# A kernel of two transformer blocks on one core: the order of rope, outputs and first projections in the second block's mixers, and the output's second quarter

## The chip, the cores and the metric

The kernel runs on one core of one Trainium2 chip. It is one program for five engines that work side by side and wait for each other through semaphores: TensorE (PE in the profile) multiplies matrices, VectorE (DVE) and ScalarE (ACT) do the elementwise work, GpSimd (POOL) does a little of it, and SyncE (SP) starts the transfers. The metric is the time of one execution on the device in microseconds, taken as the median of several runs.

## What is computed

The input is 256 tokens of width 1024 in fp32. A first block applies, each with a norm and a modulation, a feed-forward net (width 2816), a mixer (half pooling, half attention with ALiBi) and a second such net. A second block has two attention mixers with rotary embedding (rope), grouped keys and a gate z: one with a window of 128 and sinks, one that for 256 tokens is plain causal attention. The parts that the change touches:

```python
def second_block(x, norm_g, w_in_a, sinks_a, w_in_b, w_out, final_g):
...
    for i in range(DEPTH_2):
        hn = rmsnorm_2(h, norm_g[i])
        j = i // N_MIXERS
        if i % N_MIXERS == 0:
            q, k, v, z = split_proj(hn, w_in_a[j], N_KV_A)
            q, k = apply_rope(q, cos, sin), apply_rope(k, cos, sin)
            o = sliding_window_sink_attention(q, k, v, sinks_a[j])
        else:
            q, k, v, z = split_proj(hn, w_in_b[j], N_KV_B)
            q, k = apply_rope(q, cos, sin), apply_rope(k, cos, sin)
            o = moba_attention(q, k, v)
        o = o.reshape(B, S, MIX_WIDTH) * jax.nn.silu(z)
        h = h + o @ w_out[i]
    return rmsnorm_2(h, final_g)
```

## The kernel before

**Split products.** fp32 accuracy is had from three fast products. Each operand is a high part (`whi`, `nhi`, `yhi`: a rounded copy made by ScalarE) and a low part (`wlo`, `nlo`, `ylo`: the difference, made by VectorE). `split_product` issues hi x hi, hi x lo and lo x hi, so a chunk of 128 rows costs three matmuls with 256 columns.

**Weight units.** Weights come as units of 1024 x 256 (1 MB, `load_unit`, L412) into three slots. For each unit ScalarE makes the high half (`high`, L599) and VectorE the low half (`low`, L907); the next load into a slot waits for the low half of its unit. Units are numbered in the order in which they are used; a call `low(u + NS)` prepares the unit three places on. Queues are in order: an engine that waits holds up all that is behind it.

**The plan.** `mixer_plan` writes out for each mixer ("pool", "window", "causal") a list of steps, and each engine walks the same list and does its part of each step:

- K, KV, V, Q, Z, U, W: projections ("jobs") of a unit into the bank `acc[p % 2]`, 48 matmuls on TensorE; ScalarE copies the bank out (`kraw`, `vv`, `qraw`, tanh of z) and counts `job_out`.
- ROTK, ROTQ: TensorE multiplies with the rotation matrix (`rotate`, L1503 and L1506), VectorE combines with cosine and sine (`rope`, L1063 to L1067) and counts `rope_done`. For keys ScalarE then spreads the heads (`duplicate`, L709) and counts `kd_done`.
- SC: the scores of four heads (L1522, L1523), maxima on VectorE (`masked_max`, L1081), exponentials on ScalarE (L725), divisions on VectorE (`divide`, L1101). Between them lie the scaling and the gating of z (L1182, L1188). At the end ScalarE makes a high half and VectorE its low half.
- TPV: transposes of the probabilities (L1532), copies by ScalarE (`probT`, L732), products with the values (L1546, L1549), and for two pairs of heads `og` on VectorE (L1114), `yhi` on ScalarE (L743), `ylo` on VectorE (L1119) (`outputs`). ScalarE ends the step with a high half.
- OUTA, OUTB, OUT1 to OUT3: the output projection in four quarters. OUTA is chunks 0 to 5 of the first quarter, done before the last TPV, OUTB its chunks 6 and 7 after it. OUT1 to OUT3 are whole quarters of 48 matmuls. After each quarter VectorE adds the residual (L918 or L921), and in "window" ScalarE and VectorE make `nhi`, `sq` and `nlo` (L947) of the next mixer's input.
- ROW, MOD (only "pool"): parts of the modulation vector; ROW29 is a matrix row that VectorE copies (L1013) and MOD28 sums.

For the second and third mixer the order before is

```
window: KV0 Q0 ROTK ROTQ Z0 SC0      causal: K0 V0 Q0 ROTK ROTQ Z0 SC0
both:   for i in 1..3: Q(i) TPV(i-1) ROTQ Z(i) SC(i);  OUTA TPV3 OUTB OUT1 OUT2 OUT3
```

TensorE does the first half of Z, two heads' scores, then the second half, and the other two heads' scores. It also does the transposes of two heads in the middle of the next Q, and the rotation inside TPV. In "window" VectorE also computes the first block's final norm in place, as one reciprocal after SC0 (`plain_inverse`, L967) and four chunks each after SC1 and SC2 (`first_output`, L972). `token_columns` (TensorE) and `token_column` (VectorE, `rcol`) turn the norm's factors into columns, by which ScalarE scales the values `vv`.

## Time and profile before

| | |
|---|---|
| median of the runs | 813.81 us (811.53 to 816.93, 3 runs) |
| the profiled execution, its time | 816.46 us |
| the profiled execution, its span | 814.7 us |
| TensorE busy | 743.1 us, 91% |
| VectorE busy | 544.3 us, 67% |
| ScalarE busy | 367.9 us, 45% |
| GpSimd busy | 128.5 us, 16% |
| mean granted clock of TensorE | 0.951 of full speed |

"pool" runs from about 250 to 362 us of the span, "window" from 560 to 682, "causal" from 682 to the end. A busy time is the sum of an engine's instructions; matmuls overlap, so a busy TensorE need not be at its peak. The timeline lists instructions by their start with their length; a number in brackets at a row's end is the idle time of the engine just before it and the instruction that ended that idle time. The granted clock is a share of 2.4 GHz.

### The profile page before, as it was taken

How to read it: one execution, taken by the hardware profiler on the slowest of the kernel's cores; microseconds unless marked ns; L12 is line 12 of the kernel's file. 1: busy time of each engine (PE TensorE's matmuls, PEld its weight loads, DVE VectorE, ACT ScalarE, POOL GpSimd, SP SyncE). 2: the span in 40 equal slices, each digit the busy share in tenths (PEclk: the TensorE clock that was granted, in tenths of full speed). 3: DMA queues.
4: the chain of work that ended last, by engine and by line, in shares of the span. 5: the costliest groups of instructions: out<-in, count | busy, mean ns of one | idle time of the engine just before them, and what ended most of it. 6: DMA issues, size and time to landing. Idle time of an engine off the chain costs nothing.

```text
span 814.7 us, 14918 instructions
## 1 busy us (share of the span) xinstructions
PE 743.1 (91%) x6112; PEld 693.3 (85%) x6112; DVE 544.3 (67%) x783; ACT 367.9 (45%) x564; POOL 128.5 (16%) x81
## 2 busy tenths in 40 slices
PE   5799999999978998879999999999988889899984
PEld 4489999999967987669999999999877769787884
DVE  3598978877767348466478457456888856577841
ACT  3253434343434345425443434438655556356532
POOL 0052213222241805030004000004000000000000
PEclk9699999999978999798999999999999979899998
DMA  9987799777657965354667656554333315434201
GB/s 312 349 277 256 239 367 298 235 246 242 221 180 225 342 225 166 104 188 126 204 207 257 206 158 203 180 180 132 127 105 104 104 53 179 134 103 135 72 2 51
DMA packets 132455, 152.64 MB, mean 187 GB/s; under 512 B 2616, under 2 KB 126268, under 8 KB 132284
## 3 DMA queue, kind: packets, MB, share of 16 engines
q1 hardware_dynamic: 132324, 152.01, 57.5%
q8 instruction: 31, 0.51, 0.3%
q14 instruction: 12, 0.10, 0.0%
q10 hardware_dynamic: 88, 0.02, 0.0%
HBM read 150.97 MB, written 1.05 MB: 187 GB/s over the span
## 4 chain that ended last, share of the span: by engine, by line
PE 37%; DVE 9%; ACT 7%; issue 4%; DVEq 0%; ACTq 0%
PE sc L1336 5%; PE sc L1338 5%; PE sc L1337 5%; PE acc L1336 5%; PE acc L1338 5%; PE acc L1337 5%; ACT whi L599 2%; ACT prob L725 1%; DVE prob L1081 1%; DVE wlo L907 1%; PE acc L1589 1%; ACT probT L732 1%; PE acc L1591 1%; PE acc L1590 1%; PE stat L1347 1%
## 5 line engine op out<-in xcount | busy, mean ns | idle before, releaser
L907 DVE TENSOR_TENSOR wlo<-raw,whi 128x2048 fp32r<-128x2048 f32 x105 | 260.8, 2487 | 121.1 <-ACT whi L599 120.9
L599 ACT ACTIVATE whi<-raw 128x2048 fp32r<-128x2048 f32 x105 | 200.2, 1908 | 74.7 <-PE sc L1338 56.7
L1336 PE MATMUL sc<-nhi,whi 128*128 128x256 f32 x704 | 200.0, 284 | 6.0 <-DVE nlo L940 4.1
L1337 PE MATMUL sc<-nlo,whi 128*128 128x256 f32 x704 | 198.5, 282 | 0.0
L1338 PE MATMUL sc<-nhi,wlo 128*128 128x256 f32 x704 | 198.4, 282 | 0.0
L1336 PEld LDWEIGHTS sc<-nhi,whi 128*128 128x128 f32 x704 | 134.0, 190 | 7.4 <-issue 4.5
L1337 PEld LDWEIGHTS sc<-nlo,whi 128*128 128x128 f32 x704 | 135.6, 193 | 0.0
L1338 PEld LDWEIGHTS sc<-nhi,wlo 128*128 128x128 f32 x704 | 134.4, 191 | 0.0
L1336 PE MATMUL acc<-nhi,whi 128*128 128x256 f32 x376 | 112.8, 300 | 3.1 <-DVE nlo L940 2.7
L517 POOL TENSOR_TENSOR ada<-ada,cpad 128x2048 f32<-128x2048 f32 x16 | 73.0, 4569 | 243.0 <-DMA ada<-in_w_ada_dram 243.0
L1337 PE MATMUL acc<-nlo,whi 128*128 128x256 f32 x376 | 107.3, 285 | 0.0
L1338 PE MATMUL acc<-nhi,wlo 128*128 128x256 f32 x376 | 107.3, 285 | 0.0
L1336 PE MATMUL acc<-hhi,whi 128*128 128x256 f32 x320 | 89.7, 280 | 0.0
L1337 PE MATMUL acc<-hlo,whi 128*128 128x256 f32 x320 | 89.6, 280 | 0.0
L1338 PE MATMUL acc<-hhi,wlo 128*128 128x256 f32 x320 | 89.6, 280 | 0.0
L1336 PEld LDWEIGHTS acc<-nhi,whi 128*128 128x128 f32 x376 | 74.1, 197 | 12.9 <-issue 10.5
L1337 PEld LDWEIGHTS acc<-nlo,whi 128*128 128x128 f32 x376 | 74.1, 197 | 0.6 <-issue 0.5
L1338 PEld LDWEIGHTS acc<-nhi,wlo 128*128 128x128 f32 x376 | 73.8, 196 | 0.0
L983 DVE TENSOR_REDUCE macc<-ada 128x256 f32<-128x2048 f32 x16 | 61.5, 3863 | 3.5 <-POOL ada L517 3.5
L1337 PEld LDWEIGHTS acc<-hlo,whi 128*128 128x128 f32 x320 | 60.9, 190 | 0.0
L1338 PEld LDWEIGHTS acc<-hhi,wlo 128*128 128x128 f32 x320 | 60.3, 189 | 0.0
L1336 PEld LDWEIGHTS acc<-hhi,whi 128*128 128x128 f32 x320 | 60.1, 188 | 0.0
(209 smaller groups left out, 1162.5 us busy)
## 6 DMA issues: line engine op xcount, KB each, us to landing
ada<-in_w_ada_dram SPq DMA_DIRECT2D x28, 1024.0 KB, 5.2
raw<-in_w_gate_dram SPq DMA_DIRECT2D x22, 1024.0 KB, 5.9
raw<-in_w_up_dram SPq DMA_DIRECT2D x22, 1024.0 KB, 5.6
raw<-in_w_down_dram SPq DMA_DIRECT2D x22, 1024.0 KB, 4.9
raw<-in_w_out_dram SPq DMA_DIRECT2D x12, 1024.0 KB, 5.1
raw<-in_w_in_b_dram SPq DMA_DIRECT2D x10, 1024.0 KB, 5.1
raw<-in_w_in_a_dram SPq DMA_DIRECT2D x9, 1024.0 KB, 5.3
raw<-in_w_in_dram SPq DMA_DIRECT2D x8, 1024.0 KB, 7.8
```

Of the source, the lines that this page charges most:

```text
L517: nc.gpsimd.tensor_tensor(to, to, c_mul, ALU.mult).then_inc(prod_done, 1)
L599: nc.scalar.activation(whi[:, u % NS], raw[:, u % NS], ACT.Copy).then_inc(hi_done, 1)
L725: ins = nc.scalar.activation(prob[:, s, lo:up], prob[:, s, lo:up], ACT.Exp, bias=nm[:, s, b:b + 1], accum_out=den[:, s, b:b + 1])
L732: nc.scalar.activation(probT[:, h % 2], tp[h % 2][:, 0:SW], ACT.Copy).then_inc(pt_done, 1)
L907: nc.vector.tensor_tensor(wlo[:, u % NS], raw[:, u % NS], whi[:, u % NS].bitcast(F32), ALU.subtract).then_inc(lo_done, 1)
L983: nc.vector.tensor_reduce(macc[:, slot], ada[:, slot].rearrange("p c n -> p n c"), AX_X, ALU.add).then_inc(macc_done, 1)
L1081: ins = nc.vector.tensor_tensor_reduce(out=prob[:, s, lo:up], in0=sc[h % 2][:, lo:up], in1=mask[:, lo:up], scale=1.0, scalar=NEG, op0=ALU. ...
L1336: mm(to, stat_hi, mov_hi, start=first, stop=False, skip_group_check=True)
L1337: mm(to, stat_hi, mov_lo, start=False, stop=False, skip_group_check=True)
L1338: return mm(to, stat_lo, mov_hi, start=False, stop=last, skip_group_check=True)
L1347: mm(ss_ps, ones[:, :], src, start=first, stop=last).then_inc(ss_done, 1)
L1589: mm(to, yhi[:, ch, tok], hi[:, ch], start=False, stop=False, skip_group_check=True)
```

## The change

It has four parts.

1. The rope of queries that follows a TPV step stands on VectorE ahead of that step's outputs instead of behind them. The low half that followed the rope (`low(query["u"] + NS)`) stands in SC after the first two maxima. In "window" the reciprocal and the rescaling stand ahead of SC's last low half instead of behind it.
2. "window" begins KV0 ROTK Q0 ROTQ: the key rotation waits on a semaphore of its own (`k_out`, counted by the copy of the keys), and VectorE's rope of the keys stands ahead of `rcol` and the low half.
3. "causal" begins K0 Q0 ROTK V0 ROTQ: units Q0 and V0 are exchanged, the token columns move into V0, and two low halves stand behind the query's rope.
4. A new step OUTC, chunks 0 to 5 of the output's second quarter, stands between OUTA and the last TPV in all three mixers. OUT1 keeps chunks 6 and 7.

```diff
@@ mixer_plan
-                     "MOD26", "ROW28", "W0", "W1", "V1", "SC0", "Q1", "TPV0", "SC1", "OUTA", "TPV1", "OUTB", "ROW29",
+                     "MOD26", "ROW28", "W0", "W1", "V1", "SC0", "Q1", "TPV0", "SC1", "OUTA", "OUTC",
+                     "TPV1", "OUTB", "ROW29",
...
-            order = ["KV0", "Q0"] if name == "window" else ["K0", "V0", "Q0"]
-            order += ["ROTK", "ROTQ", "Z0", "SC0"]
+            order = ["KV0", "ROTK", "Q0"] if name == "window" else ["K0", "Q0", "ROTK", "V0"]
+            order += ["ROTQ", "Z0", "SC0"]
...
-            order += ["OUTA", "TPV3", "OUTB", "OUT1", "OUT2", "OUT3"]
+            order += ["OUTA", "OUTC", "TPV3", "OUTB", "OUT1", "OUT2", "OUT3"]
...
-                st["rcol"] = name != "pool" and kind == "Q" and i == 0
+                st["rcol"] = kind == {"pool": "", "window": "Q", "causal": "V"}[name] and i == 0
@@ scalar: job, mixer
-                    nc.scalar.activation(kraw[:, 0], bank[:, 0:S], ACT.Copy)
+                    nc.scalar.activation(kraw[:, 0], bank[:, 0:S], ACT.Copy).then_inc(k_out, 1)
...
-                    elif st["kind"] == "ROTK":
+                    elif st["kind"] == "ROTK" and name == "causal":
                         duplicate(st)
+                    elif st["kind"] == "ROTQ" and name == "window" and before["kind"] == "Q":
+                        duplicate(PLANS[name][1])
@@ vector: mixer
-                    if kind == "V" and name == "causal" or kind == "Q" and name == "window" and st["rcol"]:
+                    if st.get("rcol"):
                         token_column(MIX_NORM[name])
+                        if name == "window":
+                            low(st["u"] - 1 + NS)
                     if st.get("first") and name != "pool":
                         token_scales(MIX_NORM[name])
-                    if st.get("job"):
+                    if kind == "KV" or kind == "V" and name == "causal":
+                        pass
+                    elif st.get("job"):
                         job(st)
-                    elif kind in ("ROTK", "ROTQ"):
+                    elif kind == "ROTK":
                         rope(st)
-                        if kind == "ROTQ":
-                            low(query["u"] + NS)
+                    elif kind == "ROTQ" and query["i"] == 0:
+                        rope(st)
+                        low(query["u"] + NS)
+                        if name == "causal":
+                            low(query["u"] + 1 + NS)
                     elif kind == "SC":
                         masked_max(st, 0)
                         masked_max(st, 1)
+                        if before["kind"] == "Z" and before["i"]:
+                            low(query["u"] + NS)
...
+                        if name == "window" and before["i"] == 0:
+                            plain_inverse()
+                        elif name == "window" and before["i"] < 3:
+                            first_output(range(4 * before["i"] - 4, 4 * before["i"]))
                         low((before if before["kind"] in ("Z", "V") else query)["u"] + NS)
-                        if name == "window":
-                            if before["i"] == 0:
-                                plain_inverse()
-                            elif before["i"] < 3:
-                                first_output(range(4 * before["i"] - 4, 4 * before["i"]))
                     elif kind == "TPV":
+                        if st["next"]["kind"] == "ROTQ":
+                            rope(st["next"])
                         outputs(st)
@@ tensor: out_step
-                    if kind == "OUT" and st["zs_all"]:
+                elif kind == "OUTC":
+                    pe.wait_ge(lo_done, st["u"] + 1)
+                    pe.wait_ge(job_out, st["jobs"])
+                    if st["zs_all"]:
                         pe.wait_ge(z_done, st["zs_all"])
...
-                if kind == "OUTB":
-                    out_product(st, 0, 0, late, False, True).then_inc(delta, 1)
-                    out_product(st, 0, 1, late, False, True).then_inc(delta, 1)
+                if kind == "OUTC":
+                    out_product(st, 1, 0, early, True, False)
+                    out_product(st, 1, 1, early, False, False)
+                    return
+                if kind == "OUTB" or j == 1:
+                    out_product(st, j, 0, late, False, True).then_inc(delta, 1)
+                    out_product(st, j, 1, late, False, True).then_inc(delta, 1)
```

How the instructions move is seen in each engine's queue. VectorE in "window", from the last division of SC2 on to the next scores, before:

```order
L1101 TENSOR_SCALAR prob<-prob,rden 128x256
L907 TENSOR_TENSOR wlo<-raw,whi 128x2048 [waits hi_done]
L972 SCALAR_TENSOR_TENSOR hT<-hT,gainT,sq 128x256 x4
L1114 SCALAR_TENSOR_TENSOR og<-acc,sz 128x256 [waits ylo_done,pv_done]
L1119 TENSOR_TENSOR ylo<-og,yhi 128x256 [waits yhi_done]
L1114 SCALAR_TENSOR_TENSOR og<-stat,sz 128x256 [waits ylo_done,pv_done]
L1119 TENSOR_TENSOR ylo<-og,yhi 128x256 [waits yhi_done]
L1063 TENSOR_TENSOR tn<-qraw,sq 128x512 [waits rope_done,job_out]
L1066 TENSOR_TENSOR tn<-sc,sq 128x512 [waits rot_done]
L1067 TENSOR_TENSOR qT<-tn 128x512 [waits dve_step]
L907 TENSOR_TENSOR wlo<-raw,whi 128x2048 [waits hi_done]
L1081 ISA prob,mx<-sc,consts 128x128 [waits sc_done]
```

and the same place after the change, where the second low half comes ten rows on, behind the second maximum (line numbers are those of the changed file):

```order
L1108 TENSOR_SCALAR prob<-prob,rden 128x256
L976 SCALAR_TENSOR_TENSOR hT<-hT,gainT,sq 128x256 x4
L911 TENSOR_TENSOR wlo<-raw,whi 128x2048 [waits hi_done]
L1070 TENSOR_TENSOR tn<-qraw,sq 128x512 [waits rope_done,job_out]
L1073 TENSOR_TENSOR tn<-sc,sq 128x512 [waits rot_done]
L1074 TENSOR_TENSOR qT<-tn 128x512 [waits dve_step]
L1121 SCALAR_TENSOR_TENSOR og<-acc,sz 128x256 [waits ylo_done,pv_done]
L1126 TENSOR_TENSOR ylo<-og,yhi 128x256 [waits yhi_done]
L1121 SCALAR_TENSOR_TENSOR og<-stat,sz 128x256 [waits ylo_done,pv_done]
L1126 TENSOR_TENSOR ylo<-og,yhi 128x256 [waits yhi_done]
L1088 ISA prob,mx<-sc,consts 128x128 [waits sc_done]
```

The rescaling (`hT`) went ahead of the low half, and the three instructions of the rope ahead of the four of the outputs. VectorE at the start of "causal", from the sine table on, before:

```order
L957 TENSOR_TENSOR sq<-consts,rstd 128x256 [waits dve_step]
L907 TENSOR_TENSOR wlo<-raw,whi 128x2048 [waits hi_done,dve_step]
L962 COPY rcol<-stat 128x2 [waits rcol_sum]
L907 TENSOR_TENSOR wlo<-raw,whi 128x2048 [waits hi_done]
L1063 TENSOR_TENSOR tn<-kraw,sq 128x512 [waits rope_done,job_out]
L1066 TENSOR_TENSOR tn<-sc,sq 128x512 [waits rot_done]
L1067 TENSOR_TENSOR kraw<-tn 128x512 [waits dve_step]
L1063 TENSOR_TENSOR tn<-qraw,sq 128x512 [waits rope_done,job_out]
L1066 TENSOR_TENSOR tn<-sc,sq 128x512 [waits rot_done]
L1067 TENSOR_TENSOR qT<-tn 128x512 [waits dve_step]
L907 TENSOR_TENSOR wlo<-raw,whi 128x2048 [waits hi_done]
```

and after:

```order
L961 TENSOR_TENSOR sq<-consts,rstd 128x256 [waits dve_step]
L911 TENSOR_TENSOR wlo<-raw,whi 128x2048 [waits hi_done,dve_step]
L1070 TENSOR_TENSOR tn<-kraw,sq 128x512 [waits rope_done,job_out]
L1073 TENSOR_TENSOR tn<-sc,sq 128x512 [waits rot_done]
L1074 TENSOR_TENSOR kraw<-tn 128x512 [waits dve_step]
L966 COPY rcol<-stat 128x2 [waits rcol_sum]
L1070 TENSOR_TENSOR tn<-qraw,sq 128x512 [waits rope_done,job_out]
L1073 TENSOR_TENSOR tn<-sc,sq 128x512 [waits rot_done]
L1074 TENSOR_TENSOR qT<-tn 128x512 [waits dve_step]
L911 TENSOR_TENSOR wlo<-raw,whi 128x2048 [waits hi_done] x2
```

One low half went from ahead of the keys' rope to behind the queries'. TensorE at the end of "window", where the last product of OUTA is followed by the transposes of TPV3, before:

```order
L1338 MATMUL acc<-yhi,wlo 128x256
L1532 MATMUL tp<-consts,prob 128x128 [waits pt_done,p_done]
L1532 MATMUL tp<-consts,prob 128x128 x2
L1532 MATMUL acc<-consts,prob 128x128 [waits pt_done,p_done]
L1532 MATMUL acc<-consts,prob 128x128 x2
L1546 MATMUL acc<-probT,vv 64x256 [waits og_done,pt_done]
```

and after, the end of OUTA and the first rows of OUTC, which has 36 such rows ahead of the same transposes:

```order
L1355 MATMUL acc<-yhi,wlo 128x256
L1353 MATMUL acc<-yhi,whi 128x256 [waits z_done,job_out,lo_done]
L1354 MATMUL acc<-ylo,whi 128x256
L1355 MATMUL acc<-yhi,wlo 128x256
L1353 MATMUL acc<-yhi,whi 128x256
```

The 36 products came from OUT1, behind OUTB, and took its wait for `z_done` with them.

## Rows read from the trace of the kernel before

**Rows 1.** Busy time by stretch: stretch, length, PE, PEld, DVE, ACT, POOL, granted clock, DMA
```profile
620.00:660.00 40.00, 31.79 (x242) 26.77 (x244) 31.96 (x97) 22.24 (x58) 0.00 (x0) 0.91 0.27 89
...
740.00:780.00 40.00, 37.02 (x307) 31.45 (x306) 31.71 (x88) 23.52 (x53) 0.00 (x0) 1.00 0.24 80
...
648.20:652.40 4.20, 4.20 (x38) 4.20 (x37) 4.06 (x19) 2.35 (x10) 0.00 (x0) 1.00 0.47 164
...
601.00:605.30 4.30, 4.30 (x27) 3.97 (x25) 3.73 (x14) 1.60 (x8) 0.00 (x0) 0.60 0.30 89
...
656.20:666.50 10.30, 9.23 (x44) 7.24 (x45) 4.36 (x9) 4.46 (x10) 0.00 (x0) 0.52 0.32 103
```

**Rows 2.** Timeline of TensorE, matmuls behind the waits that concern the change
```profile
622.14 0.40 PE L1522 MATMUL sc<-kd,qT 64*128 64x128 f32 x2 [2.56 <-DVE qT L1067]
...
748.21 0.39 PE L1522 MATMUL sc<-kd,qT 64*128 64x128 f32 x2 [1.17 <-DVE qT L1067]
...
656.16 0.44 PE L1546 MATMUL acc<-probT,vv 128*64 128x256 f32 x2 [2.94 <-ACT probT L732]
...
328.29 0.44 PE L1546 MATMUL acc<-probT,vv 128*64 128x256 f32 x2 [3.78 <-ACT probT L732]
...
705.70 1.19 PE L1506 MATMUL sc<-qraw,consts 128*128 128x512 f32 x1 [3.50 <-issue]
```

**Rows 3.** Timeline of VectorE, a turn of its loop in "window"
```profile
613.79 2.29 DVE L907 TENSOR_TENSOR wlo<-raw,whi 128x2048 fp32r<-128x2048 f32 x1 [1.61 <-ACT whi L599]
616.00 1.67 DVE L972 SCALAR_TENSOR_TENSOR hT<-hT,gainT,sq 128x256 f32<-128x256 f32 x4
617.58 0.42 DVE L1114 SCALAR_TENSOR_TENSOR og<-acc,sz 128x256 f32<-128x256 f32 x1
...
620.07 0.69 DVE L1063 TENSOR_TENSOR tn<-qraw,sq 128x512 f32<-128x512 f32 x1
...
622.00 2.28 DVE L907 TENSOR_TENSOR wlo<-raw,whi 128x2048 fp32r<-128x2048 f32 x1
...
635.18 2.29 DVE L907 TENSOR_TENSOR wlo<-raw,whi 128x2048 fp32r<-128x2048 f32 x1 [1.61 <-ACT whi L599]
```

**Rows 4.** Timeline of VectorE, a turn of its loop in "causal"
```profile
741.45 2.29 DVE L907 TENSOR_TENSOR wlo<-raw,whi 128x2048 fp32r<-128x2048 f32 x1 [1.80 <-ACT whi L599]
...
746.15 0.69 DVE L1063 TENSOR_TENSOR tn<-qraw,sq 128x512 f32<-128x512 f32 x1
...
748.08 2.28 DVE L907 TENSOR_TENSOR wlo<-raw,whi 128x2048 fp32r<-128x2048 f32 x1
...
759.89 2.29 DVE L907 TENSOR_TENSOR wlo<-raw,whi 128x2048 fp32r<-128x2048 f32 x1 [1.80 <-ACT whi L599]
```

**Rows 5.** Timeline of ScalarE, the high half behind the outputs in "causal"
```profile
745.68 1.90 ACT L599 ACTIVATE whi<-raw 128x2048 fp32r<-128x2048 f32 x1
```

**Rows 6.** Timeline of VectorE, residuals of two output quarters in "window"
```profile
671.24 0.76 DVE L918 TENSOR_TENSOR hT<-acc,hT 128x256 f32<-128x256 f32 x2 [0.36 <-PE acc L1338]
...
677.34 0.75 DVE L918 TENSOR_TENSOR hT<-acc,hT 128x256 f32<-128x256 f32 x2
```

**Rows 7.** Timeline of VectorE and GpSimd behind the outputs of "pool"
```profile
336.70 0.88 DVE L921 SCALAR_TENSOR_TENSOR hT<-acc,mod,hT 128x256 f32<-128x256 f32 x2 [2.38 <-PE acc L1338]
...
342.07 0.42 DVE L1013 COPY macc<-tp 128x256 f32<-128x256 f32 x1
...
347.69 5.26 DVE L907 TENSOR_TENSOR wlo<-raw,whi 128x2048 fp32r<-128x2048 f32 x1 [2.29 <-ACT whi L599]
...
347.18 3.62 POOL L517 TENSOR_TENSOR ada<-ada,cpad 128x2048 f32<-128x2048 f32 x1
```

**Rows 8.** Timeline of VectorE at the start of "window"
```profile
571.62 2.29 DVE L907 TENSOR_TENSOR wlo<-raw,whi 128x2048 fp32r<-128x2048 f32 x1
573.83 0.15 DVE L962 COPY rcol<-stat 128x2 f32<-128x2 f32 x1
```

**Rows 9.** Timeline of TensorE, the first scores of "causal"
```profile
712.05 0.39 PE L1522 MATMUL sc<-kd,qT 64*128 64x128 f32 x2
```

50 lines of the change are left out of this document (30 added, 20 removed).

## The prediction

> **What bounds the kernel now.** I read the busy shares of stretches first. While the heads of the two later mixers run, TensorE is busy 79 to 93% and VectorE 79 to 80% [rows 1]: no engine is full, so what matters is the chain of waits. Its pieces alternate there between VectorE and ScalarE, and TensorE shows only as the one that waits at its end. Next I read the timeline of TensorE for the longest idle times [rows 2]. Five kinds concern this change: the scores of a group of heads wait 2.6 us for `qT` in "window" (three such waits, 2.8, 2.6, 2.6) and 0.5 to 1.2 us in "causal" (three); the first value products of `TPV3` wait 2.94 us for `probT` in "window", those of `TPV1` in "pool" 3.78 us; and the rotation of the first queries in "causal" waits 3.50 us. Behind the longest of these the granted clock fell to the lower of its two levels, 1.2 GHz: it is 0.52 of full speed over 656.2 to 666.5 and 0.60 over 601.0 to 605.3, where 27 matmuls took 4.3 us, against 38 in 4.2 us at full clock [rows 1]. A wait of 2.6 us brought this in one of two places, 2.8 and more each time.
>
> Then I asked what `qT` waits for, in the timeline of VectorE [rows 3, 4]. One turn of its loop in "window" is: the low half of weights (2.29), the rescaled residual (1.67), two outputs each with a round trip to ScalarE (2.5), the rope (1.95), another low half (2.3), four maxima and divisions. The next turn begins 21.4 us later (613.79 and 635.18). In "causal" without the rescaling it is 18.44 us (741.45 to 759.89). Inside a turn VectorE stands still for 1.6 to 1.8 us until ScalarE has made the high half [rows 3, 4] and shorter at some other places. So the loop is VectorE and ScalarE in series, and TensorE's waits are its symptom. This decides the sum: taking a wait from TensorE gives its full length only where the loop gets shorter as well.
>
> **The heads of "window".** Two things move. The rescaling (1.67 us, twice; once a reciprocal of 1.75) now stands ahead of the low half, where VectorE idled 1.61 us [rows 3]: its cover is the high half on ScalarE, and if that cover were gone it would cost its 1.67 us again. The rope stands ahead of the outputs, so `qT` is ready 2.2 + 1.95 = 4.2 us behind the start of the low half, instead of 8.3 (613.79 to the scores at 622.14). TensorE then has the rotation (it needs `qraw`, which follows the high half), the value products (0.9) and half of Z (2.8) to do, and reaches the scores about 5.1 us after the low half began, without a wait: the 2.6 us are gone. The outputs come 1.95 us later. Behind them, on ScalarE, are `yhi`, a high half of 1.9 us and then the exponentials [rows 5]. And the low half of the next-but-one weights stands between the maxima and the first division. It waits for that high half, which ends about when the maxima end (outputs + 0.3 + 1.9 against outputs + 1.6): no new wait of more than 0.5. The turn is then 2.2 + 1.95 + 2.55 + 1.5 + 2.3 + the rest of 8.3 (21.4 less all these and about 1 us of waits) = 18.8 us: 2.6 less per full turn. From the first rope on I get: scores of the second group 3.1 us earlier, the loop behind it 2.8 earlier, 5.4 after the second turn and 7.6 when ScalarE begins the high half ahead of `probT` of the fourth. So this part gives 7.6.
>
> **The last wait of "window".** `OUTC` is 36 products. 38 take 4.2 us [rows 1], so it is 4.1 us. It starts once Z3 is gated, which is about when `OUTA` ends, and it lies in the 3.7 us that TensorE now spends on transposes and waiting [rows 2]: transposes and `probT` then cost 0.4 us of lateness. Without a wait of 2.9 us the clock should stay at 2.4 GHz: now 44 matmuls behind it keep TensorE busy for 9.2 us at 0.52 [rows 1]; they would need about half, of which the round trips to ScalarE and VectorE hide part, so I take 2.5 us as the gain. Together: 7.6 - 0.4 + 2.5 = 9.7 us at the end of `OUTB`. `OUT1` then has 12 products, 1.4 us, instead of 48, 5.5 us. But this does not give 4.1 us. Each output quarter costs VectorE and ScalarE 6.1 us in series (residual 671.24, next 677.34 [rows 6]), TensorE only 5.5. The first projection of "causal" needs the last `nlo`, which comes 3 x 6.1 + 2.2 us behind the first residual: 21.4 us from `OUTB` to its end, against 22.8 now (4 x 48 matmuls at 5.5 and some of them at the lower clock). So 1.4 us, and TensorE waits about 2.8 us in K0 instead. Sum up to K0: **11.1**.
>
> **"pool".** `OUTC` fills the 3.78 us, and the clock should hold: `OUTB` ends 2.3 us earlier with 4.1 us of `OUT1` done. Here too something else is late next. `MOD28` needs the copied row of `ROW29`, which VectorE makes 5.4 us behind the residual's start (336.70 and 342.07 [rows 7]); TensorE comes there 2.3 us after `OUTB` and waits 3.6. After that VectorE's next low half again meets GpSimd's product (5.26 us instead of 2.29, [rows 7]) and `ROW31` waits behind it as before. By this chain `ROW31` is at 349.5 instead of 353.5: **3.8**. That VectorE and GpSimd hinder each other is in the row; the Trainium skill, "GPSIMD Engine Reference", section "Specifications", says that GpSimd shares its SBUF interfaces with VectorE and contends with VectorE instructions of two SBUF inputs; by that rule the collision comes again, and the trace agrees (5.26 us). If it fell away, `ROW31` would wait for the end of `OUT2` alone and the term would be 5.7.
>
> **First keys and queries.** In "window" the low half (2.29) stood ahead of the copy of `rcol`, for which ScalarE's `vv` and so the rotation waited [rows 8]. Now the rope of the keys (1.3) stands there instead, and the rotation of the keys runs ahead of Q0. Of the 2.3 us the rope takes 1.3 back, so ROTQ starts earlier by **1.0**. In "causal" TensorE now does V0 between the two rotations. The key rope no longer stands behind a second low half, so it ends at about 697.4, long before V0 does, and the query's rotation follows V0 without the 3.50 us [rows 2]. Counted from the end of K0, the scores come at 705.1 instead of 712.05 [rows 9]: 6.9 for TensorE, 1.6 of it for the clock. VectorE however has two low halves (4.5 us) behind the query's rope, so the maxima start at 708.4 instead of 713.0, which is 1 us behind the scores: 4.6 for the loop. The turns of "causal" have no rescaling to hide; permuted, they take 18.15 us against 18.44, two turns give 0.6. At the last group's scores the rope's new place helps TensorE once, 1.6 us (scores 5.15 us behind the low half instead of 6.77). 4.6 + 0.6 + 1.6 = 6.8, and 0.2 for the end, where `OUTC` meets only waits of 0.6 to 0.9 us inside the attention step, which stay. **7.0**.
>
> **Sum.** 3.8 + 1.0 + 11.1 + 7.0 = 22.9. Against it one dropped clock at K0 or MOD28: 27 matmuls in 4.3 us, which take 3.0 at 38 in 4.2 [rows 1], is a loss of 1.3; at somewhat better than even odds I take 0.9. That leaves 22.0 off a span of 814.7, an execution of 816.46: 794.5. This execution lay 0.3% above the median of the runs, 813.81; on that the forecast is **792**.
>
> **Bounds.** Lower bound of the gain: only what TensorE's first two parts give and nothing in the loops (3.8 + 1.0 + 1.4 + 4.6 less two clock drops of 1.3) is 8. Upper: every wait above gone with its clock loss, 8.0 + 2.9 + 3.8 + 3.5 + 2.8 + 1.2, and 6.9 for the clock in four stretches (1.3 in a short one, 2.5 in the longest) is 29.
>
> **Rivals.** A: TensorE is the bound and the waits go in full, 29 us, about 785. For it: TensorE has the largest busy share. Against it: VectorE's turn, which barely gets shorter in "causal". The Trainium skill, "Perfetto Trace Analysis", section "Identifying the Most-Contended Engine", tells one to work on the engine of the highest occupancy; by that rule the whole 29 us would come. The rows on VectorE's turn speak against it. Chance 0.08.
> B: the loop in "window" doesn't shorten by 2.6 a turn but by under 1, because the high half ahead of the exponentials (1.9 us, [rows 5]) is late and VectorE's low half and division wait for it; TensorE's wait moves to the transposes. Then the loops give 3 instead of 7.6 and the clock still drops: gain 9 to 15, 799 to 805. Chance 0.15.
> C: within 1%: B, and the 4.6 of "causal" are not reached because the two low halves wait for their high halves; gain 4 to 8, about 808. Chance 0.08.
> D: slower. The one mechanism is that same low half ahead of the first division: it makes all six groups wait for ScalarE's high half in series with the exponentials. It decides once it adds over 3.5 us to each turn, over seven groups 24 us and more; by the rows it is 0.1 to 0.5. About 822. Chance 0.03.
> The forecast itself, 787 to 799, has 0.66. The range of 785 to 804 takes in most of A and B. From the cases: faster by over 1% 0.88, within 1% 0.09, slower 0.03; 1% is about what a measurement of this kernel tells from no change.
>
> **What would show it.** Right: in "window" no wait for `qT` over 0.5 us and 18.8 us from one low half behind the divisions to the next, 18.1 in "causal"; no granted clock of 0.5 in the last heads of "pool" and "window"; a new wait of about 3.6 us at `MOD28` and one near 2.8 us in K0. Wrong: turns still of 21 us, or an idle VectorE ahead of the low half that now precedes the first division. If K0's wait is missing, my 6.1 us per quarter was not the bound there.

## The result, and the profile after

| | before | after |
|---|---|---|
| median of the runs | 814.54 us (811.53 to 816.93, 4 runs) | 796.50 us (795.86 to 796.62, 4 runs) |
| the profiled execution, its time | 816.46 us | 795.86 us |
| its span | 814.7 us | 793.9 us |
| TensorE busy | 743.1 us, 91% | 733.2 us, 92% |
| VectorE busy | 544.3 us, 67% | 542.9 us, 68% |
| mean granted clock | 0.951 | 0.970 |

After to before is 0.9765 (95% interval 0.9737 to 0.9792): the change makes the kernel 2.3% faster. The forecast was 792 us with a range of 785 to 804, so it lies 4.5 us low and the range holds the time. On the profiled executions, against which the sum was made, the forecast was 794.5 and the time is 795.86. (The median before, 814.54, is of the three runs behind the 813.81 and one more.)

The table below cuts both spans at the same instructions. Each number is the difference of two start times in the timeline of TensorE: the first product of ROW28 ("pool"), the first product behind "pool", the first sum of squares of "window", the first scores of SC0 and of SC3, the first sum of squares behind OUT3 of "window" (the end of K0), the first scores of "causal", its SC3, and the end of the span. The 0.9 us that was forecast for a dropped clock has a row of its own; where a clock did drop, its cost lies in the row of its stretch.

| stretch, us | before | after | gained | forecast |
|---|---|---|---|---|
| start to ROW28 (nothing changed) | 296.07 | 296.54 | -0.5 | 0 |
| ROW28 to the end of "pool" | 71.39 | 68.08 | 3.3 | 3.8 |
| up to "window" (nothing changed) | 198.43 | 198.40 | 0.0 | 0 |
| first projections of "window" | 14.72 | 13.73 | 1.0 | 1.0 |
| "window", SC0 to SC3 | 62.92 | 54.71 | 8.2 | |
| SC3 to the end of K0 | 43.83 | 42.00 | 1.8 | |
| both together | 106.75 | 96.71 | 10.0 | 11.1 |
| end of K0 to the scores of "causal" | 24.69 | 18.55 | 6.1 | |
| "causal", SC0 to SC3 | 54.61 | 53.98 | 0.6 | |
| SC3 to the end | 48.04 | 47.91 | 0.1 | |
| these three together | 127.34 | 120.44 | 6.9 | 7.0 |
| a dropped clock | | | | -0.9 |
| span | 814.7 | 793.9 | 20.8 | 22.0 |

The busy shares by stretch, of after. Columns: stretch, length, PE, PEld, DVE, ACT, POOL, granted clock, DMA share, GB/s.

```profile
600.00:640.00 40.00, 37.53 (x309) 32.05 (x308) 36.21 (x113) 23.77 (x62) 0.00 (x0) 1.00 0.37 123
720.00:760.00 40.00, 38.86 (x319) 33.52 (x318) 31.84 (x90) 23.42 (x54) 0.00 (x0) 1.00 0.25 80
340.90:346.40 5.50, 5.47 (x32) 4.19 (x33) 3.22 (x3) 2.55 (x3) 4.40 (x3) 0.50 0.01 3
...
650.80:655.00 4.20, 4.20 (x36) 4.20 (x37) 1.72 (x4) 3.38 (x7) 0.74 (x1) 1.00 0.04 12
```

and, of before, the stretch that lies to the last scores of "window" as the first row does:

```profile
612.00:652.00 40.00, 34.89 (x276) 29.57 (x275) 32.52 (x93) 21.33 (x53) 0.00 (x0) 0.96 0.32 106
```

In the heads of "window" VectorE is now busy 91% of the time and TensorE 94% at full clock; before it was 81% and 87%. (The 80% and 79% of [rows 1] are of a stretch that reaches into the last attention step.) Behind the last attention step of "window" the clock is 1.00 (last row of after), where it was 0.52 [rows 1]. It is down behind MOD28, for 32 matmuls in 5.5 us (third row).

The timeline of VectorE, of after, one turn in "window" and the marks of a turn in "causal" (they answer [rows 3, 4]):

```profile
603.83 0.55 DVE L1108 TENSOR_SCALAR prob<-prob,rden 128x128 f32<-128x128 f32 x2
604.77 0.16 DVE L1105 TENSOR_TENSOR den<-den,esink 128x2 f32<-128x2 f32 x1 [0.40 <-ACT prob L727]
...
605.63 1.67 DVE L976 SCALAR_TENSOR_TENSOR hT<-hT,gainT,sq 128x256 f32<-128x256 f32 x4
607.32 2.29 DVE L911 TENSOR_TENSOR wlo<-raw,whi 128x2048 fp32r<-128x2048 f32 x1
609.53 0.68 DVE L1070 TENSOR_TENSOR tn<-qraw,sq 128x512 f32<-128x512 f32 x1
...
611.46 0.42 DVE L1121 SCALAR_TENSOR_TENSOR og<-acc,sz 128x256 f32<-128x256 f32 x1
612.36 0.43 DVE L1126 TENSOR_TENSOR ylo<-og,yhi 128x256 fp32r<-128x256 f32 x1 [0.48 <-ACT yhi L745]
...
615.57 2.28 DVE L911 TENSOR_TENSOR wlo<-raw,whi 128x2048 fp32r<-128x2048 f32 x1
...
626.17 2.29 DVE L911 TENSOR_TENSOR wlo<-raw,whi 128x2048 fp32r<-128x2048 f32 x1
...
722.66 2.29 DVE L911 TENSOR_TENSOR wlo<-raw,whi 128x2048 fp32r<-128x2048 f32 x1 [1.80 <-ACT whi L601]
...
740.69 2.29 DVE L911 TENSOR_TENSOR wlo<-raw,whi 128x2048 fp32r<-128x2048 f32 x1 [1.80 <-ACT whi L601]
```

The low half at 607.32 has no bracket: the rescaling fills what was a wait of 1.61 us [rows 3]. The rope stands between it and the first output, and the turn's second low half, at 615.57, waits for nothing. From 607.32 to 626.17 a turn is 18.85 us, before 21.39. In "causal", with nothing to put into the wait of 1.80, it is 18.03 against 18.44.

The timeline of TensorE, of after, the waits that stand where those of [rows 2] stood, and two new ones:

```profile
646.18 0.65 PE L1568 MATMUL acc<-probT,vv 128*64 128x256 f32 x4 [0.63 <-ACT probT L734]
...
329.11 0.65 PE L1568 MATMUL acc<-probT,vv 128*64 128x256 f32 x4 [0.63 <-ACT probT L734]
...
612.62 0.50 PE L1544 MATMUL sc<-kd,qT 64*128 64x128 f32 x4
...
340.93 1.01 PE L1383 MATMUL acc<-ones,macc 128*128 128x1 f32 x4 [2.93 <-DVE macc L1017]
...
671.94 0.38 PE L1353 MATMUL acc<-nhi,whi 128*128 128x256 f32 x1 [2.35 <-DVE nlo L951]
```

The waits for `probT` went from 2.94 and 3.78 to 0.63 each, no scores wait for `qT`, and no row of "causal" has the 3.50 us. In their place TensorE waits 2.93 us at MOD28 and 2.35 us in K0; 3.6 and 2.8 were forecast.

### The profile page after: what moved, and what is told of

Its sections match the earlier page's. It is cut to its first block, busy times and chain, and to the rows that moved or that the text cites. A ratio compares the mean times of both kernels' runs of the same rounds, so it can differ in the third digit from the quotient of the medians.

```text
span 793.9 us, 14919 instructions
## 1 busy us (share of the span) xinstructions
PE 733.2 (92%) x6112; PEld 685.8 (86%) x6112; DVE 542.9 (68%) x783; ACT 366.6 (46%) x564; POOL 128.7 (16%) x81
## 4 chain that ended last, share of the span: by engine, by line
PE 68%; DVE 15%; ACT 10%; issue 4%; DMA 2%; POOL 0%; SPq 0%; DVEq 0%; ACTq 0%; POOLq 0%
PE sc L1353 10%; PE sc L1355 10%; PE sc L1354 10%; PE acc L1353 9%; PE acc L1355 8%; PE acc L1354 8%; DVE wlo L911 5%; ACT whi L601 3%; PE stat L1364 2%; DVE prob L1088 2%; DMA ada<-in_w_ada_dram 2%; ACT probT L734 1%; PE tp L1404 1%; ACT prob L727 1%; DVE prob L1108 1%
## 5 line engine op out<-in xcount | busy, mean ns | idle before, releaser
L911 DVE TENSOR_TENSOR wlo<-raw,whi 128x2048 fp32r<-128x2048 f32 x105 | 258.2, 2463 | 113.1 <-ACT whi L601 112.9
L1353 PE MATMUL acc<-nhi,whi 128*128 128x256 f32 x376 | 110.8, 295 | 5.6 <-DVE nlo L944 2.7
L1354 PE MATMUL acc<-nlo,whi 128*128 128x256 f32 x376 | 105.6, 281 | 0.0
L1355 PE MATMUL acc<-nhi,wlo 128*128 128x256 f32 x376 | 105.5, 281 | 0.0
L1353 PEld LDWEIGHTS acc<-nhi,whi 128*128 128x128 f32 x376 | 72.0, 191 | 15.2 <-issue 10.2
L1354 PEld LDWEIGHTS acc<-nlo,whi 128*128 128x128 f32 x376 | 72.1, 192 | 0.3 <-issue 0.2
L1355 PEld LDWEIGHTS acc<-nhi,wlo 128*128 128x128 f32 x376 | 71.9, 191 | 0.0
```

The source lines that it names most:

```text
L911: nc.vector.tensor_tensor(wlo[:, u % NS], raw[:, u % NS], whi[:, u % NS].bitcast(F32), ALU.subtract).then_inc(lo_done, 1)
L1353: mm(to, stat_hi, mov_hi, start=first, stop=False, skip_group_check=True)
L1354: mm(to, stat_hi, mov_lo, start=False, stop=False, skip_group_check=True)
L1355: return mm(to, stat_lo, mov_hi, start=False, stop=last, skip_group_check=True)
```

## The experiments

Eleven kernels were run, in three sessions, each session with its own runs of the kernel before (medians 816.67, 816.32 and 813.44 us). Ratios are to those, with a 95% interval. Stretches are those of the table above, each from one profiled execution. Part 2 was not run alone; its 1.0 us is read from the first projections of "window", which take 14.71 to 14.81 us in every kernel without it and 13.73 to 13.90 in every kernel with it.

**One part at a time.** The kernel before with part 4 alone:

```diff
-            order += ["OUTA", "TPV3", "OUTB", "OUT1", "OUT2", "OUT3"]
+            order += ["OUTA", "OUTC", "TPV3", "OUTB", "OUT1", "OUT2", "OUT3"]
...
```

> The kernel before with the new step OUTC alone (part 4). Theory (VectorE and ScalarE in series are the bound): in 'pool' OUTC fills the wait of 3.78 us, MOD28 then waits about 3.1 us as in the changed kernel, gain 3.0; in 'window' the wait of 2.94 us and the low clock behind it go, and K0 waits about 2.4 us, gain 5; in 'causal' 0.2. Together 8 us, ratio 0.990. Rival (all moved work is gained, 3 x 4.1, and the clock with it): 16 us, ratio 0.980. The waits of 2.6 us for qT and of 3.50 us at the first rotation of 'causal' stay.

Measured: 808.14 us, 0.9943 (0.9904 to 0.9981). Its ten times lie apart, six from 806.56 to 808.83 and four from 812.96 to 816.23, and the profiled one is among the six, so its stretches show more than the ratio does. The profiled span, 805.4, is 9.3 shorter than that of before: 4.2 from ROW28 to the end of "pool", 1.3 in the unchanged stretch behind it, 0.6 in "window", 1.75 from SC3 to the end of K0, 1.2 behind K0, where 4 matmuls run at the low clock instead of 16, and nothing at the end. The waits for `qT` stay at 2.81 and 2.54 us. Of the 5 us expected in "window" little came: OUTC alone is worth its waits in "pool" and less where the loop of VectorE sets the pace. In all, 8 us were expected; by the ratio, 0.990 lies just outside the interval.

With part 1 alone:

```diff
...
+                        if before["kind"] == "Z" and before["i"]:
+                            low(query["u"] + NS)
...
                     elif kind == "TPV":
+                        if st["next"]["kind"] == "ROTQ":
+                            rope(st["next"])
                         outputs(st)
```

The rescaling goes ahead of the low half as well, as in the change.

> The kernel before with part 1 alone (rope ahead of the outputs, the low half behind two maxima, the rescaling ahead of the low half). Theory: a turn of VectorE's loop in 'window' is 18.9 us instead of 21.4, in 'causal' 18.1 instead of 18.44; the scores no longer wait for qT; gain 7.3 in 'window' and 2.2 in 'causal', 9.5 us, ratio 0.988. The wait for probT behind OUTA and its low clock stay. Rival (TensorE is the bound, its waits for qT and the clock behind them go in full): 13.4 us, ratio 0.9835, with a turn in 'causal' of 17.1 us.

Measured: 809.35 us, 0.9918 (0.9889 to 0.9946), where 0.988 was expected; the profiled span, 809.5, is 5.2 shorter than that of before. "window" from SC0 to SC3 is 54.70 instead of 62.92 us, which is all of the 8.2 of the whole change. "causal" gets 1.5 shorter in its heads. But the last attention steps give back 1.0 and 2.0 us, so that up to K0 the 7.3 us come as expected and "causal" as a whole gives nothing instead of 2.2: SC3 to K0 takes 44.78 (43.83 before) and SC3 to the end 50.00 (48.04). The timeline of TensorE and the busy shares there, of this kernel:

```profile
650.22 0.65 PE L1550 MATMUL acc<-probT,vv 128*64 128x256 f32 x4 [3.89 <-ACT probT L732]
...
772.24 0.65 PE L1550 MATMUL acc<-probT,vv 128*64 128x256 f32 x4 [1.14 <-ACT probT L732]
...
656.50:661.20 4.70, 4.70 (x23) 4.70 (x23) 1.72 (x4) 2.90 (x7) 0.68 (x1) 0.50 0.00 0
776.90:780.70 3.80, 3.80 (x20) 3.80 (x20) 0.00 (x0) 1.90 (x1) 0.00 (x0) 0.56 0.00 0
```

A faster TensorE ahead of the last step waits longer in it (3.89 us instead of 2.94), and in "causal" a new wait of 1.14 us is followed, 4 us later, by 20 matmuls in 3.8 us at a clock of 0.56. From these rows I concluded that OUTC was worth 2 us in "causal" beside part 1, ten times the 0.2 of the prediction. That was tested below and fell.

With part 3 alone:

```diff
-            order = ["KV0", "Q0"] if name == "window" else ["K0", "V0", "Q0"]
-            order += ["ROTK", "ROTQ", "Z0", "SC0"]
+            order = ["KV0", "Q0", "ROTK"] if name == "window" else ["K0", "Q0", "ROTK", "V0"]
+            order += ["ROTQ", "Z0", "SC0"]
...
```

> The kernel before with part 3 alone (K0 Q0 ROTK V0 ROTQ in 'causal'). Theory: the first scores come 6.1 us earlier behind K0, but the maxima only 4.1 us earlier, since VectorE has two low halves behind the rope, and the loop carries 4.1 us to the end: ratio 0.995. Rival (TensorE's path counts): the 6.1 us reach the end, ratio 0.9925.

Measured: 813.66 us, 0.9977 (0.9954 to 1.0000). The scores come 6.3 us earlier behind K0 (18.36 instead of 24.69), and 1.65 of it is gone at SC3 (56.26 instead of 54.61). So 4.7 us reach the last scores: near the loop's 4.1, not TensorE's 6.1. The profiled span is only 3.3 shorter, since 0.8 was lost between SC3 and K0 and 0.6 ahead of ROW28, which the edit does not touch. The ratio shows less still, 1.9 us, and the expected 0.995 is not in its interval: that 4.7 us reach the last scores is seen in one execution, and the times alone do not show it.

**Who sets the pace.** Leave out a third of TensorE's products in the projections Q1 to Q3 and Z1 to Z3 of both mixers, 192 of them or 21.7 us, in the kernel before and in the changed one. It is the product of the weights' low part and the input's high part (the first expectation below names another); `light` is set in these projections alone, and VectorE still makes the low part:

```diff
                 mm(to, stat_hi, mov_hi, start=first, stop=False, skip_group_check=True)
+                if light[0]:
+                    return mm(to, stat_hi, mov_lo, start=False, stop=last, skip_group_check=True)
```

> The kernel before with a third of the matmuls left out of the projections Q1 to Q3 and Z1 to Z3 of 'window' and 'causal' (the product of high part and low part of the input), so its numbers are a little coarser: 16 of 48 matmuls in each of 12 units, 192 in all, 21.7 us of TensorE at full clock. Theory: the loop of VectorE and ScalarE sets the turns, which stay at 21.4 and 18.44 us less at most 0.4; TensorE's waits grow by what is left out, and more of it runs at the low clock. Gain under 4 us, ratio 0.995 to 1.0. Rival (TensorE is the bound): 20 us or more, ratio 0.975.

> The changed kernel with the same 192 matmuls left out as in the light version of the kernel before (a third of the projections Q1 to Q3 and Z1 to Z3 of 'window' and 'causal'). Theory: after the change too the loop of VectorE and ScalarE sets the turns, 18.9 and 18.1 us; gain on the changed kernel under 3 us, ratio to the kernel before 0.974 to 0.977. Rival (the change made TensorE the bound of these turns): 15 us or more, ratio 0.958.

Measured: 815.44 us, 0.9988 (0.9958 to 1.0018) for the one, 795.82 us, 0.9748 (0.9709 to 0.9787) for the other. The work that is gone turns up as waiting. The timeline of TensorE, kernel before with less TensorE work:

```profile
602.29 0.50 PE L1525 MATMUL sc<-kd,qT 64*128 64x128 f32 x4 [4.03 <-DVE qT L1067]
...
623.24 0.50 PE L1525 MATMUL sc<-kd,qT 64*128 64x128 f32 x4 [3.88 <-DVE qT L1067]
```

and the changed kernel with less TensorE work:

```profile
603.27 0.55 PE L1557 MATMUL acc<-consts,prob 128*128 128x128 f32 x3 [0.90 <-DVE prob L1108]
607.45 0.65 PE L1571 MATMUL acc<-probT,vv 128*64 128x256 f32 x4 [1.80 <-ACT probT L734]
```

The wait for `qT` grows from 2.6 to 4 us; in the changed kernel the wait is for `prob` and `probT` instead. SC0 to SC3 of "window" takes 61.96 (62.92) and 53.81 us (54.71). TensorE has the largest busy share in both kernels and bounds neither of these stretches; rival A of the prediction rested on it being the bound. That ScalarE is in the loop beside VectorE is read from VectorE's waits for it and from the next experiment; no run shortened ScalarE's own work.

**The rescaling.** The changed kernel, with reciprocal and rescaling behind the low half again:

```diff
-                        if name == "window" and before["i"] == 0:
-                            plain_inverse()
-                        elif name == "window" and before["i"] < 3:
-                            first_output(range(4 * before["i"] - 4, 4 * before["i"]))
                         low((before if before["kind"] in ("Z", "V") else query)["u"] + NS)
+                        if name == "window":
+                            if before["i"] == 0:
+                                plain_inverse()
+                            elif before["i"] < 3:
+                                first_output(range(4 * before["i"] - 4, 4 * before["i"]))
```

> The changed kernel with one thing undone: reciprocal and rescaling of 'window' (1.75, 1.67, 1.67 us on VectorE) stand behind the low half again. Theory: they lay in VectorE's wait for ScalarE's high half and lose that cover, so three turns get longer by 1.6 us each, 5 us in all, ratio 0.9825. Rival (the gain came from the rope's place alone, the rescaling is hidden either way): under 1 us, ratio 0.9765.

Measured: 801.49 us, 0.9812 (0.9777 to 0.9847). SC0 to SC3 of "window" takes 58.47 us instead of 54.71. The timeline of VectorE of this kernel has the wait back:

```profile
612.28 2.29 DVE L911 TENSOR_TENSOR wlo<-raw,whi 128x2048 fp32r<-128x2048 f32 x1 [1.60 <-ACT whi L601]
614.49 1.67 DVE L976 SCALAR_TENSOR_TENSOR hT<-hT,gainT,sq 128x256 f32<-128x256 f32 x4
```

3.8 us for three places, where 5 were expected from the 1.6 to 1.7 us of each in the row: of the 8.2 us of "window", nearly half is this one exchange. The other half goes with the places of rope and second low half, which were not moved one by one. The rest of this execution's loss (2.2 us in the unchanged feed-forward stretch, 1.0 ahead of ROW28) is not from the edit; that of 1.0 between SC3 and K0 was not traced.

**MOD28.** The changed kernel, with the copy of the matrix row ahead of the low half behind OUTB, and the same for the next row:

```diff
+                        if name == "pool" and kind == "OUTB":
+                            copy_late_row(29)
+                        elif name == "pool" and st["i"] == 1:
+                            mod_out(28)
+                            copy_late_row(30)
                         if st["i"] < 3 or name == "causal":
                             low(st["u"] + NS)
...
```

> The changed kernel, and in 'pool' VectorE copies the rows of ROW29 and ROW30 and takes the sums of MOD28 before its low half of the same step, in its wait for the high half. Theory: the wait of 3.1 us at MOD28 goes and the low clock behind it too, but VectorE's residuals and low halves, one of them held up by GpSimd's product, end the stretch: gain 1 to 2 us. Rival (TensorE's wait counts in full with its clock): 4 us. Third: nothing, as the last residual is as late as before.

Measured: 796.54 us, 0.9777 (0.9748 to 0.9807), the time of the changed kernel, as the third of the expected cases had it. The wait at MOD28 is gone and ROW28 to the end of "pool" is the same 68.06 us. The timelines of VectorE, GpSimd and TensorE of this kernel say why:

```profile
342.28 5.25 DVE L911 TENSOR_TENSOR wlo<-raw,whi 128x2048 fp32r<-128x2048 f32 x1 [1.90 <-ACT whi L601]
...
350.62 5.15 DVE L911 TENSOR_TENSOR wlo<-raw,whi 128x2048 fp32r<-128x2048 f32 x1 [2.30 <-ACT whi L601]
...
350.00 3.62 POOL L519 TENSOR_TENSOR ada<-ada,cpad 128x2048 f32<-128x2048 f32 x1 [4.61 <-DMA ada<-in_w_ada_dram]
...
356.16 1.02 PE L1388 MATMUL sc<-ones,macc 128*128 128x1 f32 x4 [4.04 <-DVE macc L1017]
```

and of after, the same two low halves and the same two products of GpSimd:

```profile
343.94 5.25 DVE L911 TENSOR_TENSOR wlo<-raw,whi 128x2048 fp32r<-128x2048 f32 x1 [2.28 <-ACT whi L601]
...
343.42 3.62 POOL L519 TENSOR_TENSOR ada<-ada,cpad 128x2048 f32<-128x2048 f32 x1
...
353.90 2.29 DVE L911 TENSOR_TENSOR wlo<-raw,whi 128x2048 fp32r<-128x2048 f32 x1 [2.29 <-ACT whi L601]
...
357.02 3.62 POOL L519 TENSOR_TENSOR ada<-ada,cpad 128x2048 f32<-128x2048 f32 x1 [9.98 <-DMA ada<-in_w_ada_dram]
```

In both kernels the first product meets a low half. The second waits for the transfer of its matrix, and in this kernel it starts at 350.00 instead of 357.02, seven microseconds earlier, so the next low half meets it as well: 5.15 us instead of 2.29. (That the transfer is earlier because VectorE gave back its buffer earlier was not tested.) The saved time comes back as a wait of 4.04 us at MOD30.

**OUTC, mixer by mixer.** The changed kernel, with OUTC taken out of "causal" alone, and out of "window" alone (OUT1 is whole there again):

```diff
-            order += ["OUTA", "OUTC", "TPV3", "OUTB", "OUT1", "OUT2", "OUT3"]
+            order += ["OUTA"] + (["OUTC"] if name not in ('causal',) else []) + ["TPV3", "OUTB", "OUT1", "OUT2", "OUT3"]
```

> The changed kernel, with OUTC taken out of "causal" alone (OUT1 is whole there again); "pool" and "window" keep it. Theory: OUTC fills TensorE's waits inside the last attention step of "causal", which moving the rope has lengthened, and keeps the clock up there. The stretch from the last scores to the end of the span is then 49.9 instead of 47.9 us, as in the kernel with part 1 alone (50.0), and the kernel is 2.0 us slower than the changed one: ratio to the kernel before about 0.979. Rival, the prediction's own step: OUTC is worth 0.2 there, since the waits stay; the stretch is 48.1 and the ratio stays at 0.9765. All other stretches as in the changed kernel to 0.3 us in both theories.

> The changed kernel, with OUTC taken out of "window" alone; "pool" and "causal" keep it. Theory: in "window" OUTC is worth 2.8 us beside part 1, as the difference of the stretches from the last scores to the sums of K0 (44.78 with part 1 alone, 42.00 with the change) says; the stretch is 44.8 here, the wait for probT is back at about 3.9 us, the wait for the last low half of the input in K0 is gone or under 0.5, and the ratio is about 0.980. Rival A: OUTC is worth what it gave alone on the kernel before (1.75 us in this stretch): 43.75 and 0.9785. Rival B, the prediction's figures (transposes and probT cost 0.4, clock 2.5 and quarters 1.4): 3.5 us, 45.5 and 0.981.

Measured without it in "causal": 797.24 us, 0.9800 (0.9783 to 0.9816); SC3 to the end takes 48.54 us, against 47.91 with OUTC (within 0.2 of it in every other kernel that has both OUTC and part 1) and 50.00 with part 1 alone. The timeline of TensorE and the busy shares of this kernel, in the places of the second and fourth row of part 1 alone:

```profile
757.52 0.65 PE L1568 MATMUL acc<-probT,vv 128*64 128x256 f32 x4 [1.15 <-ACT probT L734]
...
762.20:766.00 3.80, 3.80 (x32) 3.80 (x33) 0.55 (x1) 1.92 (x1) 0.00 (x0) 1.00 0.00 0
```

The wait is the same, 1.15 us against 1.14, and the clock holds: 32 matmuls in 3.8 us where it was 20. So of the 2.0 us in part 1 alone about 0.5 was work and the rest a clock that fell in that execution. My theory of 2.0 us falls; OUTC is worth 0.6 in this stretch, and the prediction's 0.2 was closer. Medians can't settle so little here (0.9800 and 0.9765 have intervals that overlap).

Without it in "window": 797.78 us, 0.9802 (0.9786 to 0.9819); SC3 to K0 takes 45.50 us instead of 42.00. That is 3.5 us, as by the prediction's own terms (rival B of the expectation). But single executions spread: with OUTC and the same code in this stretch it also took 42.17, 42.68 and 43.00 us (the last two with a clock that fell in K0), and 44.78 without OUTC in part 1 alone. So OUTC is worth 2 to 3.5 us there, and the ratio, with 0.980 and 0.981 both in its interval, does not tell the theory's 2.8 from 3.5. The wait of the input's low half in K0 is gone, and its place is taken by the wait and the clock of before, in the timeline of TensorE and the busy shares of this kernel:

```profile
646.59 1.12 PE L1568 MATMUL acc<-probT,vv 128*64 128x256 f32 x4 [3.88 <-ACT probT L734]
...
653.50:658.50 5.00, 5.00 (x25) 5.00 (x25) 1.72 (x4) 3.21 (x7) 0.73 (x1) 0.51 0.00 0
```

**Filling the waits that are left.** With one low half of "causal" moved ahead of the rope of the first queries, where VectorE waited 4.71 us:

```diff
+                    elif kind == "V" and name == "causal":
+                        low(query["u"] + NS)
...
-                        low(query["u"] + NS)
-                        if name == "causal":
+                        if name == "window":
+                            low(query["u"] + NS)
+                        else:
                             low(query["u"] + 1 + NS)
```

> The changed kernel, with one low half in "causal" moved from behind the rope of the first queries to ahead of it, into the 4.7 us in which VectorE waits for the rotation of these queries; nothing else. Theory: the first maxima come one low half (2.3 us) earlier, but the scores stand only 3 us ahead of them and the loop behind takes part of it back, so the stretches from K0 to the last scores lose 1.1 us as they did when all fills were made together: ratio about 0.975. Rival: they lose 2.1 us, and in the kernel with all fills it was another fill that took 1 us back: ratio about 0.974, with 52 us from the first to the last scores of "causal" instead of 53.98.

Measured: 793.06 us, 0.9747 (0.9731 to 0.9764). SC0 to SC3 of "causal" takes 52.91 us, 1.1 less, as the theory had it. In this execution the scores came 0.8 later behind K0 (19.31 us), where the clock was down for some matmuls, so the profile shows a gain of 0.2 over all of "causal"; the ratio shows 0.2% with intervals that overlap.

And with this fill, the copies of the MOD28 experiment, and a low half behind the last `nlo` of "window" instead of ahead of it:

```diff
+                            if st["i"] == 3:
+                                low(st["u"] - 1 + NS)
...
-                        if st["i"] < 3 or name == "causal":
+                        if st["i"] < 3 and (name, st["i"]) != ("window", 2) or name == "causal":
                             low(st["u"] + NS)
```

> The changed kernel with three low halves or copies moved into waits: the row copies of 'pool' as in the run that does them alone; in 'window' the low half of the third output step stands behind the last input low parts, which takes 2.3 us out of the chain to K0's last chunk; in 'causal' the low half of Q1's weights stands ahead of the query's rope, where VectorE waited 4.7 us for the rotation. Theory (VectorE and ScalarE in series): K0's wait of 2.35 us goes, 2.3 us; the first maxima of 'causal' come 2.1 us earlier and the loop carries it; with 1 to 2 of 'pool' 6 us in all, ratio 0.969. Rival (the waits move on): under 2 us, ratio 0.975.

Measured: 793.50 us, 0.9726 (0.9703 to 0.9749), profiled span 790.1. SC3 to K0 takes 39.57 us instead of 42.00, since the quarter that set the 6.1 us no longer has a low half in it; "causal" gets 1.1 shorter in its heads; "pool" nothing. The theory had 6 us and 0.969, outside the interval: 2.1 in "causal" and 1 to 2 in "pool" were too much. By ratio and by span it is the fastest kernel of the study, 3.8 us under the changed one by the profiled spans and 3.0 by the medians; against the kernel with the one fill, 0.9747, the intervals overlap.

## Why the prediction was right

**The bound.** Right. The pace of the heads is set by VectorE and its waits for ScalarE; 21.7 us less work on TensorE changed the time by 0.1%, within the interval, in the one kernel and by as little in the other.

**The heads of "window".** The turn was to be 18.8 us and is 18.95 and 18.85, as part 1 alone also has it. When ScalarE begins the high half ahead of the last `probT` the loop is 7.3 us ahead of where it was, counted from the first scores; 7.6 was the term. What was said to hide the rescaling does hide it. (The prediction's addends of the turn come to 18.8 only if the 1.67 of the rescaling is taken off the 21.4 too, which it does not say.)

**The last wait of "window".** The mechanism was right, its parts a little large. At the residual of OUTB the gain is 8.8 us where 9.7 was forecast, and at the end of K0 10.0 where it was 11.1. The mis-sized term is the clock: I took half of a stretch with 44 matmuls, 2.5 us. Counted in the timeline of before, 19 matmuls there follow each other at the low clock with 0.1 us more than at the full one, which is 1.9. The quarters were as forecast: residuals at 652.15, 658.18, 664.26 and 670.35, 6.03 to 6.1 us apart, and TensorE waits for the last `nlo`. From the first residual to the end of K0 it takes 21.31 us instead of 22.59, a gain of 1.3 for the forecast 1.4 (the prediction's 21.4 names only 3 x 6.1 + 2.2 = 20.5 of its addends).

**"pool".** 3.3 us instead of 3.8 (by the prediction's own 353.5 and 349.5 for ROW31 it would be 4.0). The wait at MOD28 came (2.93 instead of 3.6), and behind it the low half of 5.25 us beside GpSimd's product. That this is a chain that gives back what is put into it is shown by the copies moved ahead. The drop of the clock at MOD28 is in the 3.3: with OUTC alone and without OUTC in "causal", whose code is the same in this stretch, the clock was down for less time and the stretch took 67.2 us, which is a gain of 4.2. The busy shares of the latter, at the same place:

```profile
340.10:344.80 4.70, 4.70 (x36) 4.10 (x37) 2.41 (x3) 2.55 (x3) 3.64 (x3) 0.71 0.01 3
```

**"causal".** 6.9 us instead of 7.0, with its parts shifted: the scores 6.1 earlier behind K0 (6.9), the maxima 4.1 (4.6); the turns gave 0.8 (0.6), the last scores 1.5 (1.6: they stand 5.30 us behind the low half instead of 6.77), and 0.4 that was not forecast came in the first group. Part 3 alone shows the same: a quarter of TensorE's gain ahead of the first scores is gone at the last ones. The end gave 0.1 (0.2).

**The clock.** One dropped stretch was expected, at K0 or MOD28, with 1.3 us at better than even odds. One came, at MOD28, with 32 matmuls in 5.5 us in the row above, and none in K0. Against the two kernels in which it was shorter it cost 0.9 us, the very term. That it came out to the tenth is luck: in those two kernels it cost less there, and in one of them and in the one with the "causal" fill a drop came in K0 as well.

**The 4.5 us between 792 and 796.5.** On the executions the miss is 1.4 us (795.86 against 794.5), and that is the sum. (The unchanged start took 0.5 longer in this execution; without that it would be 0.9.) The rest is the base: I took the execution before to lie 2.65 us above its median and the one after to do the same, while it lies 0.6 below its own. A median and a profiled execution of one kernel can stand 2 to 3 us apart here, which is as much as several of the terms.

**What stays open.** The unchanged stretch of the feed-forward net takes 198.4 us in both kernels and in seven more, 197.2 in three and 200.6 in one. The 197.2 go with a shorter stretch at the low clock at its start, counted below; the 200.6 I can't explain. And OUTC's worth in "window" alone on the kernel before (1.75 us) against 2 to 3.5 beside part 1: part 1 lengthens the wait it fills from 2.94 to 3.89, which would account for 1 us; whether there is more to explain, single executions don't tell. By their ratios parts 4, 1 and 3 alone give 0.6, 0.8 and 0.2%, less together than the 2.3% of the whole; part 2's 1.0 us and OUTC in the lengthened wait are part of what is missing, and the rest was not told apart.

## What to carry to other kernels

Before you fill a wait of the busiest engine, find out which engines it waits for in a ring, and put the fill into *their* waits: moving 1.7 us of VectorE work into a wait for ScalarE gave about 1.3 us per turn, taking 21.7 us away from TensorE gave nothing. Independent matrix work ahead of the last attention step pays where the step's wait drops the clock behind it (2 to 3.5 us in "window"), and hardly where the wait is 1.1 us (0.6 in "causal"). And a stretch in which a clock fell once must be seen in a second execution before its length is put down to an edit: it led me to a theory of 2.0 us for something that is worth 0.6.

## What the runs showed of the hardware

**The same wait drops the clock in one execution and not in the next.** The first product of K0 waits 2.35 us in the changed kernel and in the one without OUTC in "causal", in the timeline of TensorE and the busy shares; of after:

```profile
671.90:674.20 2.30, 2.26 (x16) 2.18 (x17) 0.48 (x1) 2.30 (x4) 0.00 (x0) 1.00 1.02 342
```

and without OUTC in "causal":

```profile
669.27 0.38 PE L1353 MATMUL acc<-nhi,whi 128*128 128x256 f32 x1 [2.35 <-DVE nlo L951]
...
669.30:671.60 2.30, 2.30 (x12) 2.30 (x13) 0.55 (x2) 2.21 (x3) 0.00 (x0) 0.60 1.03 356
...
363.00:366.00 3.00, 3.00 (x14) 3.00 (x15) 3.00 (x9) 1.98 (x4) 0.00 (x0) 0.51 0.03 10
366.00:370.00 4.00, 4.00 (x38) 4.00 (x37) 2.49 (x6) 3.42 (x5) 0.00 (x0) 1.00 0.01 2
```

The granted clock is 1.00 there and 0.60 here. Seven kernels have this wait, of 2.35 to 2.51 us, and in two of them, this one and the one with the "causal" fill, the clock fell. Even a wait of 1.14 us came before a drop once (0.56, part 1 alone, with waits of 0.64 and 0.89 us between) and not the other time.

**How long it stays down varies too.** Behind a wait of 4.1 us at the end of "pool", the clock is down for 26 matmuls in 5.3 us in the changed kernel:

```profile
365.00:370.30 5.30, 5.30 (x26) 5.30 (x26) 4.70 (x12) 3.88 (x7) 0.00 (x0) 0.50 0.02 5
```

Without OUTC in "causal", whose code is the same up to there, it is back at 1.00 after 366.0, as the last two of its rows show, with 14 matmuls in 3.0 us before. That is the 1.2 us between 198.4 and 197.2.

**VectorE and GpSimd.** A low half of 2.29 us took 5.26 (before), 5.25 (changed kernel), 5.25 and 5.15 us (copies ahead) where it began 0.5 or 0.6 us behind the start of a product of GpSimd of 3.62 us. Each time it ended 2.15 us behind the product's end (352.95 and 350.80 before [rows 7], 349.19 and 347.04 after, 347.53 and 345.39, 355.77 and 353.62 with the copies ahead): as late as if it had begun only when the product was over. So the loss is what is left of the product, here about 3 us, whatever makes the two meet; with the copies ahead the second meeting came because the product stood 7 us earlier.
